# A decoder trunk on one core: turns of the second chunk inside the first value product, and a reordered hand-over to the experts

## The reference, cut to what matters

```
h = concatenate(meta_tokens, x)
for l in range(2):
    h = layer_norm(alpha*h + hybrid_mixer(h), ln1_g, ln1_b)
    h = layer_norm(alpha*h + moe_ffn(h), ln2_g, ln2_b)
return h[16:]

hybrid_mixer: proj = h @ w_in, split into qa, ckv, qi, ki, wi, qr, kr, vr, gr
              sparse latent attention (qa, ckv, index qi/ki/wi) and retention (qr, kr, vr, gate gr), then @ w_o
moe_ffn:      scores = sigmoid(h @ w_router); the best 4 of 8 groups, then the 8 best of 64 experts a token
              gates = chosen scores, normalised, times 2.5
              sum of gate * (silu(x @ w_gate[e]) * (x @ w_up[e])) @ w_down[e] over the chosen experts
              + the shared expert (silu(x @ ws_gate) * (x @ ws_up)) @ ws_down
```

## Time and profile before

| | us |
|---|---|
| median of 3 runs | 1487.34 |
| lowest and highest | 1483.96, 1491.04 |
| span of the profiled execution | 1480.7 |
| the profiled execution's own time | not listed apart; the median is 6.6 above its span |
| TensorE busy in the span | 1430.7 |
| DVE, ACT, POOL busy | 353.0, 254.0, 138.3 |

### The profile page before, as it was taken

How to read it: one execution, slowest core, us unless ns; L and a number is a source line. 1 busy time by engine, 2 the same in 40 slices (tenths; PEclk the granted TensorE clock), 3 DMA queues, 4 the chain that set the end, 5 groups by cost and what they waited for, 6 DMA issues and landing times. The chain is left out here.

```text
span 1480.7 us, 21355 instructions
## 1 busy us (share of the span) xinstructions
PE 1430.7 (97%) x8428; PEld 739.1 (50%) x8428; DVE 353.0 (24%) x1093; ACT 254.0 (17%) x608; POOL 138.3 (9%) x169
## 2 busy tenths in 40 slices
PE   8999999999999999999979999999999999999996
PEld 4755544444544454445437654444544554554552
DVE  0444551111111111111143435511111111111112
ACT  1243201111111111111122441011111111111110
POOL 2032111000000000000000221100000000000000
PEclk9999999999999999999989999999999999999998
DMA  9722429999999999999935224299999999999990
GB/s 331 299 97 86 172 78 380 409 407 396 400 400 402 394 400 407 406 393 399 346 139 199 94 106 171 78 388 405 410 417 415 412 413 414 409 413 414 413 398 33
DMA packets 103489, 471.66 MB, mean 319 GB/s; under 512 B 11744, under 2 KB 18080, under 8 KB 70544
## 3 DMA queue, kind: packets, MB, share of 16 engines
q1 hardware_dynamic: 91344, 442.32, 75.1%
q0 software_dynamic: 12096, 28.70, 5.5%
HBM read 484.91 MB, written 3.35 MB: 330 GB/s over the span
## 5 line engine op out<-in xcount | busy, mean ns | idle before, releaser
L614 PE MATMUL bank<-ring,region 128*64 128x256 f32 x4096 | 456.0, 381 | 1.7 <-issue 1.7
L614 PEld LDWEIGHTS bank<-ring,region 128*64 128x64 f32 x4096 | 296.9, 138 | 176.2 <-issue 39.7
L573 PE MATMUL bank<-region 128*128 128x512 f32 x512 | 267.5, 607 | 1.4 <-ACTq L1322 0.7
L652 PE MATMUL bank<-ring,region 128*64 128x512 f32 x1024 | 249.6, 608 | 2.4 <-ACT region L1141 1.4
L1532 DVE TENSOR_TENSOR region<-region,bank 128x256 f32<-128x256 f32 x64 | 27.0, 421 | 560.2 <-ACT region L1134 560.2
L1141 ACT ACTIVATE region<-bank 128x512 f32<-128x512 f32 x128 | 76.4, 597 | 474.6 <-PE bank L652 474.6
L1830 POOL DMA_INDIRECT region<-h_rows,rank_i x64 | 63.7, 995 | 919.7 <-DVE region L1511 863.8
L652 PEld LDWEIGHTS bank<-ring,region 128*64 128x64 f32 x1024 | 62.3, 136 | 162.9 <-issue 86.5
L573 PEld LDWEIGHTS bank<-region 128*128 128x128 f32 x512 | 78.1, 191 | 58.1 <-issue 54.9
L586 PEld LDWEIGHTS bank<-const,region 128*128 128x128 f32 x512 | 66.9, 195 | 69.2 <-ACT region L1125 42.7
L1134 ACT ACTIVATE region<-bank 128x256 f32<-128x256 f32 x64 | 24.6, 385 | 413.8 <-PE bank L614 413.8
(11 more groups left out here) (206 smaller groups left out, 847.6 us busy)
## 6 DMA issues: line engine op xcount, KB each, us to landing
ring<-in_w_gate_dram SPq DMA_DIRECT2D x64, 2048.0 KB, 10.4
ring<-in_w_up_dram SPq DMA_DIRECT2D x64, 2048.0 KB, 13.0
ring<-in_w_down_dram SPq DMA_DIRECT2D x64, 2048.0 KB, 9.1
ring<-in_w_in_dram SPq DMA_DIRECT2D x8, 2048.0 KB, 17.4
ring<-in_w_o_dram SPq DMA_DIRECT2D x4, 2048.0 KB, 11.0
ring<-in_w_in_dram SPq DMA_DIRECT2D x4, 1024.0 KB, 8.2
ln_par<-in_ln_g_dram POOLq DMA_DIRECT2D x4, 512.0 KB, 5.5
ln_par<-in_ln_b_dram POOLq DMA_DIRECT2D x4, 512.0 KB, 7.4
```

Of the source, the lines that this page charges most:

```text
L573: last = mm(bank[SUM_BANKS[n][half]][0:w, :], selg[:, u, t0:t0 + w], y_sb[:, u, half * 512:(half + 1) * 512], start=False, stop=stop, skip ...
L614: last = mm(bank[5][64 * e:64 * e + 64, part * F:(part + 1) * F], xgT[:, u, kk, 64 * e:64 * e + 64], w[:, e, kk, :], start=(kk == 0), stop ...
L652: last = mm(bank[6][64 * e:64 * e + 64, :], mo["h2"][:, j * 128 + 64 * e:j * 128 + 64 * e + 64], w[:, e, j, half * 512:(half + 1) * 512], ...
```

## The change

It has more parts than its title says.

- TensorE: the turns of chunk 2 stand behind the first four steps of `v1`, in both layers.
- TensorE: the turn of the lists stands ahead of the opening of the sums. The down product of chunk 2 (and of chunk 0 in layer 0) is cut into four pieces, which `round_` places in the first pair where the others have `scatter`.
- DVE: the lists are made in one go, with plain waits, ahead of the count; the shared expert's hidden rows come behind the read of the lists.
- `finish` of the mixer's norm moves from DVE to POOL, behind its powers and ahead of `memset(score)`.
- The area `xg` is written with zeros by ACT behind its `scores` and not by POOL (`rows_clear`).

Context lines that are left out are marked.

```diff
@@ -351,6 +351,7 @@
         moe_clear = sem("moe_clear")
+        rows_clear = sem("rows_clear")
         router_sums = sem("router_sums")
...
@@ -574,7 +575,7 @@
-            def round_(l, r):
+            def round_(l, r, shared_piece=None):
...
@@ -625,11 +626,15 @@
                             scatter(l, 1 - u, 1, 0)
+                        elif shared_piece:
+                            shared_piece(0)
                         if not ends:
...
                             scatter(l, 1 - u, 1, 1)
+                        elif shared_piece:
+                            shared_piece(1)
                         pe.wait_ge(h_ready, g * 32 + p + 1)
...
@@ -640,6 +645,8 @@
                                 scatter(l, 1 - u, 0, 0)
+                        elif shared_piece:
+                            shared_piece(2)
                         pe.wait_ge(ht_ready, g * 32 + p + 1)
...
@@ -655,6 +662,8 @@
                                 scatter(l, 1 - u, 2, 1).then_inc(scattered, 1)
+                            elif half == 0 and shared_piece:
+                                shared_piece(3).then_inc(scattered, 1)
...
@@ -710,10 +719,11 @@
                 turn_h(before, 1)
-                turn_h(before, 2)
                 pe.wait_ge(w_in_in[V], l * 16 + 16)
                 features_ready(before, 1)
-                project_tokens("v1")
+                project_tokens("v1", 0, 4)
+                turn_h(before, 2)
+                project_tokens("v1", 4, KC)
                 turn_h(before, 0)
...
@@ -1019,38 +1029,46 @@
-                def shared_down(n):
+                def shared_down(n, pieces):
                     t0, w = CHUNKS[n]
                     pe.wait_ge(shared_ready, SHARED[l][n])
-                    if n == 0:
-                        parts = [(o, q * 256, 256) for q, o in enumerate(meta_quads(SUM_BANKS[0][0], 256))]
-                    else:
-                        parts = [(bank[b][0:w, :], half * 512, 512) for half, b in enumerate(SUM_BANKS[n])]
-                    for j in range(2):
+                    for at in pieces:
+                        if n == 0:
+                            j, parts = at, [(o, q * 256, 256) for q, o in enumerate(meta_quads(SUM_BANKS[0][0], 256))]
+                        else:
+                            j, half = at // 2, at % 2
+                            parts = [(bank[SUM_BANKS[n][half]][0:w, :], half * 512, 512)]
                         for o, c0, cols in parts:
...
+                pe.wait_ge(score_ready, SCORED[l])
+                if l == 0:
+                    pe.wait_ge(shared_sig, SHARED[l][0])
+                turn_lists(l * ROUNDS)
                 pe.wait_ge(h_ready_tok, NORM[(l, 0)][2])
-                pe.wait_ge(ws_down_in, l * 16 + 16)
                 open_sums(1)
...
                 turn_hidden(2)
-                shared_down(1)
-                pe.wait_ge(score_ready, SCORED[l])
-                turn_lists(l * ROUNDS)
+                pe.wait_ge(ws_down_in, l * 16 + 16)
+                shared_down(1, range(4))
                 if l == 0:
...
                     open_sums(0)
-                last = shared_down(2)
-                if l == 0:
-                    last = shared_down(0)
-                last.then_inc(scattered, 1)
                 hold_here(pe, count_ready, l + 1)
                 most = pe.value_load(count_i[0:1, 0:1], min_val=0, max_val=T)
-                round_(l, 0)
+                pe.wait_ge(shared_ready, SHARED[l][QUERIES[l][0] if l == 0 else 2])
+                def shared_piece(at):
+                    last = shared_down(2, [at])
+                    if l == 0 and at >= 2:
+                        last = shared_down(0, [at - 2])
+                    return last
+                round_(l, 0, shared_piece)
                 last_sums(l, 0, sums_done, SUMMED[l][SUM_ORDER[l][-1]])
...
@@ -1276,7 +1294,7 @@
                     act.wait_ge(router_done, l * 2 + part + 1)
-                    act.wait_ge(moe_clear, l * 2 + 2)
+                    act.wait_ge(moe_clear, l + 1)
                     for n in ns:
...
@@ -1285,6 +1303,8 @@
                 scores([2], 1)
+                act.wait_ge(const_in, 16)
+                act.activation(mo["xg"], const[:, 0:2 * ROW], ACT.Copy, scale=0.0).then_inc(rows_clear, 1)
...
@@ -1432,15 +1452,11 @@
                 normalise(l, 0, 1)
-                if l == 0:
-                    finish(l, 0, 0)
                 stats(l, 0, 2)
...
                 rows_to_features((l, 0), 2)
-                finish(l, 0, 1)
-                finish(l, 0, 2)
...
@@ -1492,6 +1508,16 @@
+            def first_lists(l):
+                left, at = mo["left"][0:64, FIRST[l]:T], l * ROUNDS * (CAP // 4)
+                for j in range(CAP // 8):
+                    eight = mo["list"][0:64, 8 * j:8 * j + 8]
+                    dve.max(eight, left).then_inc(list_step, 1)
+                    dve.wait_ge(list_step, at + 2 * j + 1)
+                    dve.match_replace(left, eight, left, 0.0).then_inc(list_step, 1)
+                    dve.wait_ge(list_step, at + 2 * j + 2)
             def read_lists(g):
...
@@ -1516,7 +1542,8 @@
                 if shared_hidden:
-                    shared_hidden(0)
+                    for n in SHARED[l]:
+                        shared_hidden(n)
                 turned(0, 0)
...
@@ -1752,20 +1779,17 @@
-                shared_hidden(1)
                 dve.wait_ge(chosen_turned, l + 1)
...
                                          ALU.mult, ALU.mult).then_inc(left_ready, 1)
+                dve.wait_ge(left_ready, l + 1)
+                first_lists(l)
                 step(dve.tensor_reduce(mo["cmax"][0:1, :], bank[4][0:1, 448:512], AX, ALU.max))
...
                 dve.tensor_copy(count_i[0:1, :], mo["cmax"][0:1, :]).then_inc(count_ready, 1)
-                dve.wait_ge(left_ready, l + 1)
-                make_lists(l, l * ROUNDS, 0, 5)
-                shared_hidden(2)
-                make_lists(l, l * ROUNDS, 5)
                 hold_here(dve, count_ready, l + 1)
                 most = dve.value_load(count_i[0:1, 0:1], min_val=0, max_val=T)
-                round_(l, 0, False, shared_hidden if l == 0 else None)
+                round_(l, 0, False, shared_hidden)
                 with dve.If(most > CAP):
...
@@ -1817,6 +1841,17 @@
                         .then_inc(ln_rstd_ready, 1)
+            def finish(l, n):
+                rows = slice(0, CHUNKS[n][1])
+                pool.wait_ge(ln_par_in, (2 * l + 1) * 32)
+                pool.wait_ge(xhat_act, NORM[(l, 0)][n])
+                if n:
+                    pool.wait_ge(xhat_dve, NORM_HALF[(l, 0)][n])
+                step(pool.tensor_tensor(h_tok[rows, n, :], xhat[0][rows, n, :], ln_par[rows, 0, :], ALU.mult))
+                after_steps()
+                pool.tensor_tensor(h_tok[rows, n, :], h_tok[rows, n, :], ln_par[rows, 1, :], ALU.add).then_inc(h_ready_tok, 1)
...
@@ -1884,14 +1919,15 @@
                 layer_norm(l, 0)
+                for n in QUERIES[l]:
+                    finish(l, n)
                 pool.memset(mo["score"], 0.5).then_inc(moe_clear, 1)
-                pool.memset(xg[:, :, :], 0.0).then_inc(moe_clear, 1)
                 for n in QUERIES[l]:
...
                 load_ln(l, "ln2_g", "ln2_b")
-                pool.wait_ge(moe_clear, l * 2 + 2)
+                pool.wait_ge(rows_clear, l + 1)
                 pool.wait_ge(h_stored, (48, 80)[l])
...
```

## The result

| us | before | changed |
|---|---|---|
| median of 16 runs each | 1488.36 | 1491.87 |
| lowest, highest | 1482.62, 1491.24 | 1490.35, 1494.46 |
| ratio (95% interval) | | 1.0032 (1.0021 to 1.0043) |
| span of the profiled execution | 1480.7 | 1490.8 |

The changed kernel is 0.3% slower: +3.5 us where I had forecast +11.9. Yet the two profiled executions are 10.1 us apart.

What follows compares the result with a forecast made beforehand. TensorE, busy 1430.7 of 1480.7 us, was taken as the bound. Starts -1.7 and +1.4, hand-overs +5.0 and +0.6, clock +6.6 summed to +11.9 us on the median 1487.3: 1499.2 us, range 1487 to 1506.

Steps and rivals of the forecast that it cites:

- I add the sum to the median: Final step: the sum of terms, +11.9 us, put on the runs' median of 1487.3, not the profiled span of 1480.7.
- the clock's term: Half clock behind new TensorE gaps at the hand-overs: +2.65 and 1.3 us in layer 0, +2.65 in layer 1.
- rival 1: The clock recovers at once or doesn't fall behind the new gaps: +5.3 us only, 1492.6; chance 18%.
- start of layer 0: v1 starts at 8.1 us, its first four steps ahead of chunk 2's turns: -1.7 us.
- start of layer 1: Chunk 2's turns, hidden in a wait before, now stand inside v1: +1.4 us, between +0.9 and +2.6.
- gaps ahead of the lists: TensorE idle at both hand-overs until DVE's lists are made: 3.5 us in layer 0, 5 us in layer 1.
- opening pair after: First pair of experts, its gaps filled by down-product pieces: 16.9 us in layer 0, 15.9 us in layer 1.
- The path through POOL: Hand-over: POOL's products delay memset, sigmoid and logits' turn; TensorE's shared block +7.25 us in layer 0, +2.5 in layer 1.
- The lists' order: Lists' turn moved ahead of the sums at the hand-over: TensorE idles 3.5 us in layer 0, 5 us in layer 1.
- Rival 2: POOL's products cost no more than DVE's, 1.2 us: 1482.8, or 1486.7 with clock lost in list gaps; chance 12%.
- Rival 3: More lost at half clock, three 6.4 us stretches and a late return at layer 1's start: 1503.5 us; chance 18%.
- Rival 4: Only the title's change counts, the hand-over being hidden somewhere: -0.3 us, 1487.0; chance within that of rival 2.

Runs made afterwards that it cites:

- after_dve_finish: The changed kernel with the norm's scale and offset back on DVE, all else as changed: 1487.22 against 1487.05 us for the kernel before, ratio 0.9996.
- title_only: The kernel before with only the turns of chunk 2 inside v1, in both layers: 1487.26 against 1487.14 us, ratio 0.9992.
- pool_finish_only: The kernel before with only scale and offset moved to POOL ahead of the memset, and xg's zeroing to ACT: 1493.69 against 1487.14 us, ratio 1.0046.
- b_look5: The kernel before, unchanged, one more profiled execution: span 1489.8 us, mean clock 0.983.

## Why the prediction was wrong, point by point

The direction was right, the size was not. **The step that failed is "I add the sum to the median", and with it the clock's term, "Together +6.6".** The sum was made against one execution that had spent the least at half clock, and was then set on a median of executions that spend more. Of the 6.6 us by which "the median of the runs is 1487.3, 6.6 more" than the span, about 1.8 lie outside the span in every run of this kernel; 4.8 were the luck of that execution.

Against that one execution the clock's term was right: in the changed kernel's trace the half clock behind the three new gaps costs 2.6, 1.7 and 3.0 us, some 7.2 in all. But a typical run of before has a mean clock of 0.9873 and the changed kernel has 0.9872, and the two traces of the changed kernel with 21.0 and 19.4 us of work at half clock lie among those of before with 14.5 to 33.2. The row of "a gap of 2.4 us" at full clock holds in 6 of the 14 traces and not in the other 8. Against a typical execution the change costs no half clock on balance.

The 8.4 us between +11.9 and the measured +3.5 divide so. The two profiles are 10.1 us apart, so 1.8 us are terms that were mis-sized. The profiled execution of before is 4.2 us quicker than the mean of 35 runs and that of the changed kernel 0.7 us slower than the mean of its 16; that leaves 5.2. The rest, 1.7, is mostly that the 16 runs of before beside the changed kernel have a median 1.2 us above that of the 35.

What is left of my sum without the clock's term, +5.3, gives 1492.6, rival 1's number, and 1491.87 was measured. That this is so near is partly luck, and rival 1's reason isn't right: the clock does fall behind the new gaps. Nor is the +5.3 free of the clock. It counts as gained the 1.6 and 3.0 us of half clock that leave the opening pairs, and as lost 0.5 us of it in layer 1's start. Without these it is +9.4, and span times clock has +4.9. Nearly half of what I had for the work itself was thus too much, for the most part in the POOL path and behind the lists: 1.65 and 1.25 us at the blocks of shared products, behind POOL (next table). A further 0.9 and 1.3 us are what stands between the turn of the lists and the gate product (13.15 and 13.36 us measured, 1.65 and 3.0 of it half clock, where I had added up 12.4 and 11.7 at full clock).

The other terms, profile against profile:

| term | forecast | measured |
|---|---|---|
| start of layer 0 | -1.7 | -1.1 |
| start of layer 1 | +1.4 | +2.0 (first turn to `v2` 14.45 against 12.44) |
| block of shared products, layer 0 | +7.25 | +5.6 (190.45 - 185.97, start's -1.1 taken out) |
| the same, layer 1 | +2.5 | +1.25 (936.50 - 926.18, less 9.07 that it came with) |
| gaps ahead of the lists | 3.5, 5.0 | 3.4, 4.8 |
| opening pair after | 16.9, 15.9 | 17.05, 15.94 |
| gate product with its clock, layer 0 | +9.0 | +6.7 (5.6 and the start's 1.1) |
| the same, layer 1 | +5.75 | +3.5 (12.54 less 9.07) |
| wait for TensorE's own instructions | 0 | +1.4, by execution |

The starts, the gate products, the opening pairs (+0.04 and -2.4 against before) and the last row add up to the 10.1 us between the profiles.

- **The path through POOL** was right as a mechanism, and the experiments that take it out and put it in alone show it (5 to 6 us, and 5 us by span times clock). Its six operations were mis-sized: 1.99 and 2.34 to 2.41 us in turn where I had 2.36 for each and 2.45 with the gap, so 13.2 us and not 14.7 from the first to the last. The multiplication is the short one and the addition the long one; the earlier trace rows has one kind of row for each width and could not show it.
- **The start of layer 0** lost 0.6 of its gain. `v1` does start at 7.83, but its steps are slow at first, by the timeline of its weight loads:

```profile
8.82 0.33 PEld L706 LDWEIGHTS bank<-ring,hT 128*128 128x128 f32 x1 [0.52 <-issue]
9.67 0.33 PEld L706 LDWEIGHTS bank<-ring,hT 128*128 128x128 f32 x1 [0.52 <-issue]
10.53 0.33 PEld L706 LDWEIGHTS bank<-ring,hT 128*128 128x128 f32 x1 [0.52 <-issue]
11.35 0.19 PEld L706 LDWEIGHTS bank<-ring,hT 128*128 128x128 f32 x1 [0.49 <-issue]
11.78 0.19 PEld L706 LDWEIGHTS bank<-ring,hT 128*128 128x128 f32 x1 [0.24 <-issue]
```

A step takes 0.85 us until 11.4 and 0.43 behind that, twice as long for the same instruction, as at 1.2 and 2.4 GHz. The page's clock line has full speed for this stretch, so that it is the clock is argued, not shown. In the kernel before the same time fell mostly on the wait for the transfer; the turns there, at 9.24, took 1.97 us where later ones of their size take 1.05, so they were slow as well.
- **The lists' order** was right within 0.2 us in both layers. It gives with one hand and takes with the other: the new place of the lists, the pieces and the starts together come to nothing (`after_dve_finish`).
- **Rival 2** (POOL as quick as DVE, not slower) didn't happen, but its times for a hand-over without the wait, 1482.8 and 1486.7, stand near the 1485.6 and 1487.2 of the two kernels that take the wait out. **Rival 3** fell: by the mean clocks the change has no more half clock than before. **Rival 4** fell with `title_only` and `pool_finish_only` together: the title's change can't be told from nothing, and the hand-over through POOL alone has the whole slowdown.
- The chance of "same" was 0.25; +0.3% is within the 0.5% that I had named, so the likelier answer was put at slower with 0.70.

What stays open: why the clock falls behind the same gap or product in some executions and not in others, what makes the first steps of `v1` slow, and why the changed kernel's runs spread over 4 us and those of before over 9.

## What to carry to other kernels

A profile is one execution. Ahead of adding a sum to a median, ask how that execution stands among the runs: a mean clock and a span for each run, or the distance of its time from the median, say whether its clock is typical. Cost a change's half clock against what a typical run already loses, not against the best one. And when work moves to an idle engine, look first at what is queued there behind it: here a memset of 0.3 us held the critical path for 5 us, and putting it first removed that wait.

## What the runs showed of the hardware that I had not expected

- The mean granted clock of one kernel's executions differs: 0.983 to 0.991, worth 10 us of 1485, by stretches at half clock at places (in `b_look5` within 72 to 78, 178 to 186, 826 to 834 us) where other executions of the same code have 1.00.
- A gap of 2.44 us on TensorE ahead of the router's product left the clock at 1.00 in the first trace of before; in `b_look5` the clock is at 0.50 from about 1 us behind the same gap (2.45 us), for some 3.4 us of work.
- POOL's multiplication of 1024 columns, `xhat` by `ln_par` into `h_tok`, takes 1.99 us, and its addition of `ln_par` to `h_tok` in place 2.35. Whether the operation or the operands make the difference is not shown.
- TensorE's wait for its own instructions between the two layers is 7.2 to 9.3 us in the traces, longer than the norm that it stands beside (in the changed kernel's trace `xhat` of chunk 1 is ready at 756.5 and the turns start at 764.8). No edit here touched it.
